# TensorE's program without loops, an earlier counter and another order of the last projection pass in a streaming encoder trunk

## The chip, the cores and the metric

The kernel runs on one core of a Trainium2 chip. Its engines are TensorE (PE; PEld is its weight load), VectorE (DVE), ScalarE (ACT), GpSimd (POOL) and SyncE (SP). The metric is the device time of one execution in microseconds (us); lower is better. TensorE's clock has two levels, 2.4 and 1.2 GHz; the profile gives the granted clock as a share of the higher one.

## What is computed

One layer of a streaming encoder for 640 tokens (512 of a prompt, 8 streams of 16), model width 2048, all in float32. Cut to what matters:

```python
xn = rms_norm(x, norm_mix_g)
glu, qkv, b_raw, a_raw, z, gates = split(xn @ w_in)
y_conv = silu(layer_norm(causal_dwconv(glu_a * sigmoid(glu_b)) + b)) @ conv_pw2
o, s_new = gated_delta_chunked(q, k, v, beta, g, s_prev, chunk)   # per 64 or 16 tokens
y_dn = (rms(o) * silu(z)) @ dn_w_o
x = x + (sigmoid(g0) * y_conv + sigmoid(g1) * y_dn) @ w_out       # the projection
xn = rms_norm(x, norm_ffn_g)
s = (xn @ w_q) . sub_keys; top 16 of 16 x 16 pairs, 8 heads       # the router
x = x + sum_k gelu(xn . u[idx_k]) * gate_k * v[idx_k]             # 16384 experts
y = rms_norm(x, norm_final_g)
```

## The kernel before, in words

Each engine has its own hand-written program; they meet only at semaphores, which count upwards. A float32 product is made of three passes of a rounded format: the operand's high part (`hi`, a copy by ScalarE) and low part (`lo`, the difference, by GpSimd or VectorE), multiplied high by high, high by low and low by high. So behind most matmuls stands a chain: a load by SyncE, `hi` on ScalarE, `lo` on GpSimd or VectorE, then TensorE.

The kernel goes through four stages.

1. **Input projections and convolutions** (from 59 us to about 690 us on TensorE): `pe.Fori(0, NC)`, L498, 8 iterations of five groups q, k, v, gate, glu, 480 matmuls of 320 columns each. `product` (L489) issues them. Then the gates' products go on as filler work.
2. **The gated delta rule**: `pe.Fori(0, PT)`, L694, 4 iterations. `delta` issues the small matmuls of one tile of 128 tokens, and `gates(n)` puts n filler matmuls between them. A last tile, for the streams, is written out behind the loop.
3. **Merge, projection, router.** `merge_half` (L1659, L1663) makes y_conv and y_dn, in a loop at L1670; VectorE's `merge` (L1929, L1931, L1935) combines them into the rows `mhi` and `mlo`, 16 rows in all, and raises `mg_out` (at L1931) and `m_lo` (at L1935). The projection goes over 8 column blocks of 256 (`oc`), two halves of the inner dimension (`kh`) and five token tiles (`t`): 7 blocks in the loop at L1692, in the order kh, high parts of all t, low parts of all t; the eighth block behind it (`for t`, L1730 and on) in the order t, kh. Its weight halves `whi[kh]`, `wlo[kh]` are one buffer each: half 0 is free again after `w_done`, half 1 after the block's last low part (`wo_mm`); ScalarE's `weight` (L1806) fills `whi` and raises `w_hi`, GpSimd (L2231) fills `wlo` and raises `w_lo`. VectorE's `add` (L1949) adds a bank to x and raises `wo_add`, which TensorE asks for before it writes that bank again. So that the first block passes, VectorE raises `wo_add` by five itself, at L1942, behind its last merge: TensorE's first projection matmul stands behind all of VectorE's merges. The router is the loop at L1786: `query` and `scores` (L1759, L1749).
4. **Experts** (from 2345 us). First one-hot products `group` with the first table's units between them (loops at L2476 and L2481), then 32 chunks in `phase`. A chunk has 8 units; TensorE's unit is 24 matmuls of 384 columns (L2467, L2472) and then 2 x 10 of the second table (L2498 in float32; L2506, L2507, L2508 in three passes), whose low weights VectorE makes (`low_v`, L2744). `phases` (L2347 and on) writes chunk 1 alone, 14 chunks in a loop of 7 iterations (L2352), chunks 16 and 17 alone, 12 chunks in a loop of 6 iterations (L2357), and the last three alone. All engines have the same shape of program. VectorE and GpSimd also gather and weight single expert rows in it (L2806, L2771), and SyncE and ScalarE load both tables.

In a loop the value that a wait asks for stands in a register. `wreg`, `Stage.count` and `wait_count` therefore wait and then also raise a counter of their own:

```python
def wait_count(eng, name, s, v):
    eng.wait_ge(s, v)
    eng.sem_inc(pace2[name], 1)
```

Of the kernel before, what the change touches and what calls it, by code (L numbers as in the profile page):

```python
# [19 lines left out]
TILES = T // P  # L20
PT = NP_TOK // P
# [3 lines left out]
NC = CONV // P  # L25
# [11 lines left out]
NOC = D // OCW  # L37
# [32 lines left out]
CHUNKS = NK // ET  # L70
# [4 lines left out]
NU = 2 * ET  # L75
# [6 lines left out]
GLN, GTILE = 8, 6  # L82
NGU = H + 2 * KD
RAWMOVE = 2 * len(KINDS) * NC + 2 * GLN + 2


def build(nc, x_prompt, x_sample, consts, params, conv_prefix, dconv_prefix, state_in, w_ba, w_first, w_units,
          keys, ffn_g, final_g, peer_u, peer_v, u_units, v_units,
          y_prompt, y_sample, conv_new_p, dconv_new_p, state_new_p, conv_new_s, dconv_new_s, state_new_s):
    with ExitStack() as ctx:  # L90
# [95 lines left out]
        def wreg(eng, name, s, v):  # L186

            eng.wait_ge(s, v)
            eng.sem_inc(pace[name], 1)
# [19 lines left out]
        NPROJ = 2 * len(KINDS) * NC  # L209
# [245 lines left out]
        def _(pe):  # L455
# [39 lines left out]

            pe.wait_ge(x_hi, 2 * TILES)
            pe.wait_ge(x_lo, 2 * TILES)
            with pe.Fori(0, NC) as c:  # L498
                for i, kd in enumerate(KINDS):
                    if kd == "q":  # L500
                        pe.wait_ge(glu_done, c + 1)
                    elif kd == "v":
                        pe.wait_ge(norm_root["k"], c + 1)
                    elif kd == "gate":
                        pe.wait_ge(evac["q"], c + 1)
                    elif kd == "glu":
                        pe.wait_ge(evac["k"], c + 1)
                    for kh in range(2):
                        n = 2 * i + kh
                        pe.wait_ge(lo_done, c * 10 + (n + 1))  # L510
                        for th in range(2):
                            m = product(ps[PSK[kd]], n, kh, th, 0, 24)
                        m.then_inc(unit_done, 1)
                pe.wait_ge(sq_done["q"], c + 1)
                pe.wait_ge(norm_root["q"], c + 1)
                sum_rows(ps[3], at(SQ, T)).then_inc(mm_sum["q"], 1)
                pe.wait_ge(sq_done["k"], c + 1)
                pe.wait_ge(evac["v"], c + 1)
                sum_rows(ps[2], at(SQ + T, T)).then_inc(mm_sum["k"], 1)
# [171 lines left out]

            pe.wait_ge(ln_root, 1)
            pe.wait_ge(ln_mean, 1)
            with pe.Fori(0, PT) as t:  # L694
                gates, done = gate_steps(t * GTILE + GLN, t * (2 * GTILE) + (NPROJ + 2 * GLN), RAWMOVE, lambda s, v: wreg(pe, "pe", s, v))
                delta(t, False, lambda s, v: wreg(pe, "pe", s, v), lambda per, k: t * per + k, gates)
                assert done[0] == PER * GTILE, done
            gates, done = gate_steps(GLN + PT * GTILE, NPROJ + 2 * (GLN + PT * GTILE), RAWMOVE, lambda s, v: pe.wait_ge(s, v))
            delta(PT, True, lambda s, v: pe.wait_ge(s, v), lambda per, k: count_s(per, k), gates)
# [732 lines left out]
        class Stage:  # L1432
# [14 lines left out]
            def count(self, eng, name, s, v):  # L1447

                eng.wait_ge(s, v)
                eng.sem_inc(self.pace[name], 1)  # L1450

            def block(self):
                return self.run.enter_context(nc.Block())
# [191 lines left out]
        def _(pe, st=st):  # L1645
# [21 lines left out]
            merge_half(1, 1, 1, 1)  # L1667
            merge_half(2, 0, 0, 0, c_lo)
            merge_half(3, 1, 1, 0)
            with pe.Fori(1, MN // 2) as i:  # L1670
                for r in range(2):
                    st.count(pe, "pe", mg_out, 2 * i + r - 1)
                    for j in range(2):
                        merge_half(i * 4 + (2 * r + j), 2 * i + r, r, j)

            def weights(kh):
                return tuple(w[:, kh, :].rearrange("p (k c) -> p k c", k=8) for w in (whi, wlo))
# [11 lines left out]
            pe.sem_inc(wo_mm, TILES)  # L1689
            pe.wait_ge(m_lo, 8)  # L1690
            pe.wait_ge(mg_out, MN - 1)
            with pe.Fori(0, NOC - 1) as oc:  # L1692
                for kh in range(2):
                    wh, wl = weights(kh)
                    st.count(pe, "pe", w_hi, 2 * oc + kh + 1)
# [31 lines left out]
                        m = pe.transpose(ps[TR_BANK[n]][:, k * P:(k + 1) * P], x1[:, t, kk * P:(kk + 1) * P], ident)  # L1727
                    m.then_inc(n_tr, 1)

            for t in range(TILES):  # L1730
                pe.wait_ge(wo_add, (NOC - 1) * TILES + t + 1)
                for kh in range(2):
                    wh, wl = weights(kh)
                    pe.wait_ge(w_hi, EN - 1 + kh)
                    high(t, kh, wh)
                    pe.wait_ge(w_lo, EN - 1 + kh)
                    m = low(t, kh, wl)
                m.then_inc(wo_mm, 1)
                if t >= 2:
                    transpose(t - 2)  # L1740
            transpose(3)
            pe.wait_ge(iota_st, 2)

# [39 lines left out]
            query_rows(0, TCOLS[1:], 0, KD, False)  # L1783
            query_rows(0, TCOLS[1:], 0, KD, True).then_inc(q_mm, 1)
            query(0, 1, True)
            with pe.Fori(1, QN // 2) as i:  # L1786
                for r in range(2):
                    query(i, r, False)
            scores(QN - 1, 1)
# [118 lines left out]
        def _(v, st=st):  # L1908
            v.memset(nsm[:, 0, :], 0.0).then_inc(eps_set, 1)
            v.memset(nsm[:, 1, :], EPS).then_inc(eps_set, 1)  # L1910

            def split_low(lo, src, hi, i, s_hi, s_lo):

# [25 lines left out]
            with v.Fori(1, MN // 2) as i:  # L1939
                for r in range(2):  # L1940
                    merge(i * 2 + r, r, i * 4 + (2 * r + 2))
            v.sem_inc(wo_add, TILES)  # L1942
            v.wait_ge(xr_ld, 32)

            def add(oc, t):
# [361 lines left out]
        def wait_count(eng, name, s, v):  # L2307

            eng.wait_ge(s, v)
            eng.sem_inc(pace2[name], 1)  # L2310

        xg_ld, x1g_ld, iota_ready = sem2("xg_ld"), sem2("x1g_ld"), sem2("iota_ready")
        pre_ld, g0_ld, g_mul = [sem2(f"pre_ld{i}") for i in range(PRE)], sem2("g0_ld"), sem2("g_mul")
# [22 lines left out]
        NQ = NGG * NBB  # L2336
# [97 lines left out]
        def _(pe):  # L2434
# [38 lines left out]
                if 3 in quarters:  # L2473
                    mmi.then_inc(unit_free, 1)

            with pe.Fori(0, NU // 4) as i:  # L2476
                for u in range(4):
                    for g in range(4):
                        group(i * 16 + (u * 4 + g), g % 2)
                        first_table(i * 4 + u, u % 2, i * 2 + u // 2, u // 2, (g,))  # L2480
            with pe.Fori(0, (NQ - 4 * NU) // 2) as i:  # L2481
                for r in range(2):
                    group(i * 2 + (4 * NU + r), r)

            def phase(c, par, ut, vt, has_u):
                for j in range(NU):
# [4 lines left out]
                    for q in range(2):  # L2491
# [15 lines left out]
                            pe.matmul(out, vh, a_l, start=False, stop=False)  # L2507
                            mmi = pe.matmul(out, vl, a_h, start=False, stop=e == SPLIT - 1)  # L2508
                        mmi.then_inc(v_mm, 1)
            phases(pe, phase)  # L2510

            pe.wait_ge(v_add, CHUNKS * KD + 4)
            for t in range(DT):
# [489 lines left out]
```

## Time and profile before

| | |
|---|---|
| time, median of 3 executions | 4795.71 us (4790.95 to 4795.77) |
| the profiled execution | 4787.57 us |
| its span, first to last instruction | 4786.0 us |
| TensorE busy | 4548.3 us (95%), 28205 matmuls |
| VectorE busy | 3410.1 us (71%) |
| ScalarE, GpSimd busy | 1317.9 us, 1323.9 us |
| mean granted TensorE clock | 0.977 |
| fetched for TensorE's program (queue q8) | 136 packets, 2.23 MB |

Matmuls are pipelined, so a row's duration (0.3 us) is longer than the step from one matmul to the next. Idle time in front of an instruction is written behind its row, with what ended it; "issue" stands for time in which the engine waited for nothing that the profile shows. An engine name with a q behind it (DVEq, PEldq) is that engine's sequencer: its branches, register work and semaphore increments, which are not counted as busy.

### The profile page before, as it was taken

The numbers are of one execution on the slowest core, as the hardware profiler recorded it, in microseconds if no ns is written. First come the engines' busy times: TensorE is split into PE (matmuls) and PEld (weight loads), VectorE is DVE, ScalarE is ACT, GpSimd is POOL, SyncE is SP. The second block draws the span as 40 slices with busy tenths as digits, with TensorE's granted clock in tenths as the row PEclk, the third lists the DMA queues.
The fourth block names the chain that finished last, engine by engine and source line by source line (L and its number), as shares of the span: only waits on it lengthen the run. The fifth ranks groups of instructions, "written<-read, shape, count | busy, mean of one in ns | idle before, by whom it ended". The sixth has DMA issues, their size and how long they took to land. (4 is left out here: it accounts for less than half of the span.)

```text
span 4786.0 us, 84564 instructions
## 1 busy us (share of the span) xinstructions
PE 4548.3 (95%) x28205; PEld 4355.8 (91%) x28205; DVE 3410.1 (71%) x4571; ACT 1317.9 (28%) x2054; POOL 1323.9 (28%) x936
## 2 busy tenths in 40 slices
PE   8999989999999999999679999999999999999995
PEld 8999989999998999999678998999999999999994
DVE  4889872334443331068887988898899999999998
ACT  4232323222221221132372222222222222222222
POOL 0111132211222333333002333333333333333332
PEclk8999999999999999999899999999999999999998
DMA  3222323221224433221268999999999999999998
GB/s 119 86 87 85 88 66 98 72 70 59 73 76 155 138 115 141 88 111 65 76 221 327 370 368 356 367 367 363 364 372 380 381 376 374 378 378 374 377 377 329
DMA packets 283660, 1085.18 MB, mean 227 GB/s; under 512 B 23696, under 2 KB 104464, under 8 KB 209936
## 3 DMA queue, kind: packets, MB, share of 16 engines
q0 software_dynamic: 74752, 538.99, 28.7%
q1 hardware_dynamic: 168336, 400.91, 25.2%
q10 hardware_dynamic: 40320, 142.10, 7.6%
q8 instruction: 136, 2.23, 0.2%
q14 instruction: 116, 0.95, 0.1%
HBM read 1017.03 MB, written 64.88 MB: 226 GB/s over the span
## 5 line engine op out<-in xcount | busy, mean ns | idle before, releaser
L489 PE MATMUL ps<-xhi,hi 128*128 128x320 f32 x2560 | 773.8, 316 | 31.0 <-POOL lo L1391 15.7
L489 PE MATMUL ps<-xlo,hi 128*128 128x320 f32 x2560 | 761.8, 311 | 0.0
L2506 PE MATMUL ps<-ahi,vhi 128*128 128x384 f32 x1536 | 667.4, 434 | 45.7 <-DVE workr L2744 45.7
L2467 PE MATMUL ps<-xhi,whi 128*128 128x384 f32 x2048 | 691.9, 338 | 9.3 <-issue 9.3
L2467 PE MATMUL ps<-xlo,whi 128*128 128x384 f32 x2048 | 688.3, 336 | 0.0
L2580 ACT ACTIVATE whi<-work 128x1024 fp32r<-128x1024 f32 x240 | 254.6, 1061 | 1519.5 <-PE ps L2472 1429.0
L2806 DVE CUSTOM_DVE_ANT_0 work<-work,keep 128x2048 f32<-128x2048 f32 x256 | 585.2, 2286 | 33.1 <-DMA work<-in_peer_u,cur_u 21.8
L2771 DVE SCALAR_TENSOR_TENSOR keep<-work,act_w,keep 128x2048 f32<-128x2048 f32 x256 | 600.7, 2346 | 4.5 <-DMA work<-in_peer_v,cur_v 3.0
L2870 POOL DMA_INDIRECT work<-in_peer_v,cur_v x256 | 369.7, 1444 | 757.6 <-DVE keep L2771 729.5
L2507 PE MATMUL ps<-alo,vhi 128*128 128x384 f32 x1536 | 521.1, 339 | 0.0
L2508 PE MATMUL ps<-ahi,workr 128*128 128x384 f32 x1536 | 520.9, 339 | 0.0
L489 PEld LDWEIGHTS ps<-xhi,hi 128*128 128x128 f32 x2560 | 485.2, 190 | 36.2 <-POOL lo L1391 16.2
L489 PEld LDWEIGHTS ps<-xlo,hi 128*128 128x128 f32 x2560 | 485.3, 190 | 2.9 <-issue 2.9
L2870 POOL DMA_INDIRECT work<-in_peer_u,cur_u x256 | 248.0, 969 | 721.8 <-DVE hid L2806 696.2
L489 PE MATMUL ps<-xhi,lo 128*128 128x320 f32 x2560 | 441.9, 313 | 0.0
L2724 DVE TENSOR_TENSOR wlo<-work,whi 128x1024 fp32r<-128x1024 f32 x240 | 293.8, 1224 | 172.4 <-ACT whi L2580 156.0
L1391 POOL TENSOR_TENSOR lo<-keep,hi 128x1024 fp32r<-128x1024 f32 x80 | 211.1, 2639 | 695.9 <-ACT hi L720 685.5
L2506 PEld LDWEIGHTS ps<-ahi,vhi 128*128 128x128 f32 x1536 | 291.9, 190 | 122.1 <-issue 57.3
L2498 PE MATMUL ps<-aT,work 128*128 128x384 f32 x992 | 402.4, 488 | 0.2 <-issue 0.2
L2472 PE MATMUL ps<-xhi,wlo 128*128 128x384 f32 x2048 | 398.7, 335 | 0.0
L2467 PEld LDWEIGHTS ps<-xhi,whi 128*128 128x128 f32 x2048 | 386.0, 188 | 10.1 <-issue 10.1
L489 PEld LDWEIGHTS ps<-xhi,lo 128*128 128x128 f32 x2560 | 391.6, 189 | 1.0 <-issue 1.0
(336 smaller groups left out, 8188.9 us busy)
## 6 DMA issues: line engine op xcount, KB each, us to landing
work<-in_v_units ACTq DMA_DIRECT2D x256, 512.0 KB, 8.2
work<-in_u_units SPq DMA_DIRECT2D x240, 512.0 KB, 8.2
keep<-in_w_first SPq DMA_DIRECT2D x160, 512.0 KB, 3.6
keep<-in_w_units SPq DMA_DIRECT2D x32, 1024.0 KB, 4.9
gates_dram<-work SPq DMA_DIRECT2D x8, 3072.0 KB, 11.8
gbuf<-gates_dram SPq DMA_DIRECT2D x31, 768.0 KB, 10.2
arena<-in_w_units SPq DMA_DIRECT2D x32, 512.0 KB, 4.1
gates_T<-keep SPq DMA_DIRECT2D x32, 320.0 KB, 2.2
```

The costliest lines, as they stand in the source:

```text
L489: m = pe.matmul(out[:, o:o + HT], w[:, k, :], x[:, 8 * kh + k, c], start=kh == 0 and i == 0, stop=kh == 1 and i == 23)
L2467: pe.matmul(out, h3[:, k, :], (xlo if m % 2 else xhi)[:, 8 * half + k, :], start=half == 0 and m == 0, stop=False)
L2472: mmi = pe.matmul(out, l3[:, k, :], xhi[:, 8 * half + k, :], start=False, stop=half == 1 and k == 7)
L2498: pe.matmul(out, w4[:, q, e, :], (a0 if is_first(c) else aT[1 - par])[:, e, :], start=e == 0, stop=False)
L2506: pe.matmul(out, vh, a_h, start=False, stop=False)
L2507: pe.matmul(out, vh, a_l, start=False, stop=False)
L2508: mmi = pe.matmul(out, vl, a_h, start=False, stop=e == SPLIT - 1)
L2580: act.activation(whi[:, r, :], uraw[r], ACT.Copy).then_inc(hi_done, 1)
L2724: v.tensor_tensor(wlo[:, r, :], uraw[r], whi[:, r, :].bitcast(F32), ALU.subtract).then_inc(lo_done, 1)
L2771: v.scalar_tensor_tensor(x1g[:, t, :], row, act_w2[:, j:j + 1], x1g[:, t, :], ALU.mult, ALU.add).then_inc(v_used, 1)
L2806: v.tensor_tensor_reduce(out=row, in0=row, in1=xg[:, ut, :], scale=1.0, scalar=0.0, op0=ALU.mult, op1=ALU.add, accum_out=hid[:, j:j + 1]). ...
L2870: pool.indirect_dma_start(out=dst, out_offset=None, in_=table, in_offset=bass.IndirectOffsetOnAxis(ap=cur, axis=0)).then_inc(ld, 16)
```

## The change

Two edits. In the first, all nine loops of TensorE's program are written out by Python's `range`; the other engines keep theirs. The waits' values are then plain numbers, and for these `Stage.count` and `wait_count` no longer raise the pace counter. In the experts' stage TensorE no longer uses `phases`. In the second, VectorE raises `wo_add` by five at the head of its program for stage 3 and not behind its merges, and the projection's last block takes tiles 0 and 1 together: both with half 0 of the weights, then both with half 1.

```diff
-            with pe.Fori(0, NC) as c:
+            for c in range(0, NC):
...
-            with pe.Fori(0, PT) as t:
-                gates, done = gate_steps(t * GTILE + GLN, t * (2 * GTILE) + (NPROJ + 2 * GLN), RAWMOVE, lambda s, v: wreg(pe, "pe", s, v))
-                delta(t, False, lambda s, v: wreg(pe, "pe", s, v), lambda per, k: t * per + k, gates)
+            for t in range(0, PT):
+                gates, done = gate_steps(t * GTILE + GLN, t * (2 * GTILE) + (NPROJ + 2 * GLN), RAWMOVE, lambda s, v: pe.wait_ge(s, v))
+                delta(t, False, lambda s, v: pe.wait_ge(s, v), lambda per, k: t * per + k, gates)
...
                 eng.wait_ge(s, v)
-                eng.sem_inc(self.pace[name], 1)
+                if type(v) is not int:
+                    eng.sem_inc(self.pace[name], 1)
...
-            with pe.Fori(1, MN // 2) as i:
+            for i in range(1, MN // 2):
...
-            with pe.Fori(0, NOC - 1) as oc:
+            for oc in range(0, NOC - 1):
...
-            for t in range(TILES):
-                pe.wait_ge(wo_add, (NOC - 1) * TILES + t + 1)
-                for kh in range(2):
-                    wh, wl = weights(kh)
-                    pe.wait_ge(w_hi, EN - 1 + kh)
-                    high(t, kh, wh)
-                    pe.wait_ge(w_lo, EN - 1 + kh)
-                    m = low(t, kh, wl)
-                m.then_inc(wo_mm, 1)
-                if t >= 2:
-                    transpose(t - 2)
+            def last_half(t, kh):
+
+                wh, wl = weights(kh)
+                pe.wait_ge(w_hi, EN - 1 + kh)
+                if kh == 0:
+                    pe.wait_ge(wo_add, (NOC - 1) * TILES + t + 1)
+                high(t, kh, wh)
+                pe.wait_ge(w_lo, EN - 1 + kh)
+                m = low(t, kh, wl)
+                if kh:
+                    m.then_inc(wo_mm, 1)
+
+            last_half(0, 0)
+            last_half(1, 0)
+            last_half(0, 1)
+            last_half(1, 1)
+            for t in range(2, TILES):
+                last_half(t, 0)
+                last_half(t, 1)
+                transpose(t - 2)
...
-            with pe.Fori(1, QN // 2) as i:
+            for i in range(1, QN // 2):
...
             v.memset(nsm[:, 1, :], EPS).then_inc(eps_set, 1)
+            v.sem_inc(wo_add, TILES)
...
-            v.sem_inc(wo_add, TILES)
             v.wait_ge(xr_ld, 32)
...
-            with pe.Fori(0, NU // 4) as i:
+            for i in range(0, NU // 4):
...
-            with pe.Fori(0, (NQ - 4 * NU) // 2) as i:
+            for i in range(0, (NQ - 4 * NU) // 2):
...
-            phases(pe, phase)
+            for c in range(1, CHUNKS + 1):
+                phase(c, c % 2, None, None, c < CHUNKS)
```

## Rows read from the trace of the kernel before

**Rows 1.** The page: busy time of the engines over the span
```profile
...
PE 4548.3 (95%) x28205; PEld 4355.8 (91%) x28205; DVE 3410.1 (71%) x4571; ACT 1317.9 (28%) x2054; POOL 1323.9 (28%) x936
```

**Rows 2.** What TensorE (PE) waited for: engine, line, releaser, us in total, times, longest
```profile
...
PE ps L2506 <- DVE workr L2744: 45.7, 15, 12.6
...
PE ps L2467 <- issue: 9.3, 3, 4.2
PE ps L1682 <- DVEq L1942: 8.1, 1, 8.1
...
PE ps L489 <- issue: 5.8, 3, 2.2
...
PE ps L1749 <- issue: 1.3, 6, 0.2
```

**Rows 3.** Loop-end branches of TensorE's sequencer, of three loops: duration ns min/median/max
```profile
...
L694 PEldq COMPARE_BRANCH  x4: 83/3616/4065, 942.0 to 1367.4; - x4
...
L2352 PEldq COMPARE_BRANCH  x7: 76/208/7036, 2723.5 to 3578.8; - x7
...
L2357 PEldq COMPARE_BRANCH  x6: 76/208/223, 3854.3 to 4543.3; - x6
```

**Rows 4.** Stretches of the experts' stage: us; busy us of five engines; clock; DMA share
```profile
...
2865.10:3009.90 144.80, 139.88 (x738) 130.44 (x737) 126.52 (x128) 36.08 (x65) 47.61 (x40) 0.99 0.95 359
3292.40:3436.10 143.70, 139.45 (x737) 130.71 (x736) 126.94 (x128) 35.95 (x65) 50.51 (x40) 0.99 0.96 365
3578.80:3716.60 137.80, 137.80 (x738) 129.35 (x737) 126.77 (x128) 36.11 (x65) 50.22 (x40) 1.00 0.98 378
```

**Rows 5.** DMA queue of TensorE's instructions: whole span, then 3578.8 to 3854.3 us
```profile
...
q8 instruction: 136, 2.23, 0.2%
...
q8 instruction: 13, 0.21, 0.3%
```

**Rows 6.** TensorE's timeline: start, us, instruction, idle before it and releaser
```profile
...
1087.86 0.38 PE L489 MATMUL ps<-xhi,hi 128*128 128x320 f32 x1 [2.22 <-issue]
...
1809.17 0.55 PE L1682 MATMUL ps<-d_whi,d_mhi 128*128 128x256 f32 x1 [8.06 <-DVEq L1942]
...
2019.48 1.22 PE L1686 MATMUL ps<-d_wlo,d_mhi 128*128 128x256 f32 x8 [2.20 <-POOL d_wlo L2231]
...
2876.98 0.41 PE L2506 MATMUL ps<-ahi,vhi 128*128 128x384 f32 x1 [3.57 <-DVE workr L2744]
...
3299.98 0.41 PE L2467 MATMUL ps<-xhi,whi 128*128 128x384 f32 x1 [4.25 <-issue]
...
3442.67 0.41 PE L2467 MATMUL ps<-xhi,whi 128*128 128x384 f32 x1 [3.09 <-issue]
```

**Rows 7.** Timelines of ACT, DVE and POOL around the projection's first and last pass
```profile
...
1799.19 1.92 ACT L1806 ACTIVATE d_whi<-keep 128x2048 fp32r<-128x2048 f32 x1 [6.75 <-DMA keep<-in_w_units]
...
1802.97 3.82 DVE L1931 TENSOR_TENSOR arena<-arena 128x640 f32<-128x640 f32 x1
...
1808.86 1.91 ACT L1806 ACTIVATE d_whi<-keep 128x2048 fp32r<-128x2048 f32 x1 [1.22 <-DVE d_mlo L1935]
...
1811.12 4.59 POOL L2231 TENSOR_TENSOR d_wlo<-keep,d_whi 128x2048 fp32r<-128x2048 f32 x1 [5.02 <-ACT d_whi L1806]
...
2014.88 4.56 POOL L2231 TENSOR_TENSOR d_wlo<-keep,d_whi 128x2048 fp32r<-128x2048 f32 x1 [9.80 <-ACT d_whi L1806]
```

**Rows 8.** Two stretches behind TensorE's longest wait, columns as in Rows 4
```profile
...
1809.00:1812.50 3.50, 3.33 (x15) 3.36 (x16) 0.00 (x0) 1.77 (x1) 1.38 (x1) 0.50 1.02 433
1812.50:1815.00 2.50, 2.50 (x22) 2.50 (x22) 0.00 (x0) 0.00 (x0) 2.50 (x1) 0.99 1.01 419
```

**Rows 9.** VectorE's timeline at three loop starts of the experts' stage
```profile
...
2873.36 0.17 DVE L2760 TENSOR_TENSOR act_w<-act_w,sel 128x8 f32<-128x8 f32 x1 [3.45 <-issue]
...
3302.47 1.02 DVE L2744 TENSOR_TENSOR workr<-work,vhi 128x384 fp32r<-128x384 f32 x2
...
3445.44 1.02 DVE L2744 TENSOR_TENSOR workr<-work,vhi 128x384 fp32r<-128x384 f32 x2
```

More of the change, by code:

```diff
@@ L2309, in wait_count @@
             eng.wait_ge(s, v)
-            eng.sem_inc(pace2[name], 1)
+            if type(v) is not int:
+                eng.sem_inc(pace2[name], 1)
         xg_ld, x1g_ld, iota_ready = sem2("xg_ld"), sem2("x1g_ld"), sem2("iota_ready")
```

## The prediction

> **What bounds the kernel now.** I read the page first: TensorE is busy 4548.3 of 4786.0 us, the next engine 3410 [rows 1]. So only two things shorten the kernel: time in which TensorE stands still, and time in which it runs at the lower clock. The next view is the list of what TensorE waited for [rows 2]. The reader is to see that few of its entries have to do with loops: 9.3 us in three pieces and 5.8 us in three pieces under "issue", which is the sequencer itself; 1.3 us in six pieces under "issue" in the router; and 8.1 us at L1682, whose releaser is VectorE's sequencer at L1942, the increment that the change moves. The largest entry, 45.7 us for VectorE's low weights at L2744, is work and not program.
>
> The third view is the loop-end branch [rows 3]. TensorE's program has nine loops and 47 taken branches. A normal one takes 208 ns, while matmuls already handed over go on running, and no idle time stands behind it: in the last loop of the experts' stage all five are 208 to 223 ns, and its stretches are 137.8 us. Only six branches are long. Three are the three taken ones of the delta rule's loop (median 3.6 us, longest 4.1), three are in the first experts' loop (up to 7.0 us). They are the six "issue" pieces above.
>
> The fourth view is what straight code costs, and the trace holds that comparison already. Chunks 16 and 17 and their neighbours are written out: from 3578.8 to 3854.3 us 13 packets of TensorE's instructions were fetched [rows 5], and TensorE was busy 137.80 of 137.80 us in the stretch shown [rows 4]; the looped stretches behind it, without a fetch for TensorE, take 137.8 too. Straight and looped code run alike apart from the six branches.
>
> **The change part by part.**
>
> *Loops of the delta rule.* It removes three long branches: 5.8 us of idle time [rows 2], 2.22 of it in front of the matmul at 1087.86 [rows 6]. Behind that one the clock fell to the lower level for 3.4 us. What such a fall costs: at clock 0.50 TensorE started 15 matmuls in 3.5 us, at 0.99 then 22 in 2.5 us [rows 8], so 3.4 us at half rate lose about 1.5 to 1.7 us. Together 7.3 us. The work behind the branch is filler gate products whose weights are ready, and the small matmuls that need VectorE come 38 matmuls (5.6 us) later, so I take nothing off; the bounds are 4 and 7.5.
>
> *Loops of the experts' stage.* Three branches with 9.3 us of idle time go. But here something is late next. VectorE's program keeps its loop, and at its loop start it too stands under "issue" for 3.1 to 3.7 us before L2760 [rows 9], in every iteration. Where TensorE's branch was short, that alone made TensorE wait: 3.57 us in front of 2876.98 for L2744 [rows 6], and that iteration took 144.8 us, longer than the 143.7 with a 7 us branch in it [rows 4]. So I work out when the low weights would be asked for. A unit is 137.8 / 16 = 8.61 us, and 26 of its 46 matmul records come before the first low weights: 4.9 us. At 3299.98 TensorE had been free since 3295.73; it would ask at 3300.6. The first of VectorE's two pieces at 3302.47 ends at 3303.0, and TensorE starts 0.3 us later: a wait of 2.7 instead of 4.25 us, gain 1.5. At 3442.67 in the same way: free at 3439.6, asks at 3444.5, gets them at 3446.3, a wait of 1.8 instead of 3.09, gain 1.2. The third (free at 2727.0, weights at 2732.5) gains 0.8. The clock falls after either wait. Sum 3.5 us; the bounds are 0 and 9.3 plus two clock falls, 12.5.
>
> A rule of the Trainium skill can be held against these rows. Runtime: NRT & Kernel Launch, section Instruction fetch mechanics, says that a taken branch whose target lies outside a window of two blocks of 256 instructions forces a fetch before execution goes on, and names this as a reason to unroll. Four of TensorE's loops have bodies longer than that, with 21 taken branches; at the 2.5 us that the six cost on average the rule would give 53 us. The rows show 15 us, from six branches only, so the sum goes by the rows.
>
> *The other seven loops, the register waits and the pace counters.* A wait on a register is three steps of TensorE's sequencer and a constant one at most one, but the sequencer is ahead of the matmuls everywhere except where it waits for data. The cover is TensorE's queue of matmuls already issued. What remains is the router's 1.3 us in six pieces [rows 2]; I take 0.6, between 0 and 1.3. In the one-hot loops before the experts VectorE works without a break, so nothing is gained there.
>
> *The counter raised early.* At 1801.1 the merge's last matmul has been issued and the first weights are there (ScalarE's copy from 1799.19 takes 1.92 us, [rows 7]). TensorE then idles 8.06 us until VectorE's increment [rows 6]. What is late next? Tiles 0 to 3 need nothing more, 64 matmuls at 0.12 us are 7.7 us, until 1809. Tile 4 writes a bank that VectorE's last merge reads; its sum at 1802.97 ends at 1806.8. The low weights of half 0 were begun by GpSimd at once and take 4.6 us. Half 1 is asked for at 1801.2 + 14.4 = 1815.6 and is copied by 1810.8, its low part at 1825.2 and ready at 1815.7 [rows 7]. Nothing is late, so 8.0 us go, and with them the 3.5 us at clock 0.50 behind the idle time [rows 8], another 1.5. Sum 9.5 us; the bounds are 6 and 9.5. VectorE's increment at the head of its program is one sequencer step ahead of its first subtraction, under 0.1 us.
>
> *The last pass.* TensorE asked for half 1's low weights after two thirds of tile 0 and idled 2.20 us until 2019.48 [rows 6]; GpSimd made them from 2014.88 in 4.56 us [rows 7], and could not begin before half 1 was free, so they are due at 2019.4 after the new order too. The new order puts 24 matmuls (2.9 us) of tile 1 ahead, which moves the request from 2017.1 to 2020.0, 0.6 us behind the weights. Idle time 2.3 and one clock fall 1.5: 3.8 us. Against it, tile 0 is finished 0.5 us later than now, but its norm has until tile 2 is done. From tile 1 on everything is earlier by the full amount, the wait for the last tile's norm and transposes moves with it. The bounds are 1 and 4.
>
> Sum: 7.3 + 3.5 + 0.6 + 9.5 + 3.8 = 24.7 us. The profiled execution took 4787.57 us, which gives 4762.9. The median of the three timed runs stands 8.1 us above it; taken off the median, the sum gives 4771.0, and that is my number.
>
> **The rivals.**
>
> *Slower: every further packet of instructions costs TensorE.* 136 packets are fetched now. In the straight stretch there were 13 packets to about 2950 records of weight loads and matmuls; 56410 records make some 250, so about 110 more, half of them where the DMA engines are busy 0.95 to 0.98 of the time [rows 4]. 0.3% of 16 engines over 275.5 us is 1.0 us for each packet [rows 5]. If each delayed TensorE by that, 110 us would be lost against 24.7 gained: 4881. It decides from 0.22 us a packet on. Against it: 13 packets in that same full stretch cost nothing. For it only that packets and data share the engines. Chance 0.05.
>
> The same page of the Trainium skill calls crossing a block mostly hidden; by that, and by the trace, this rival is weak.
>
> *The removed waits come back.* In the experts' stage VectorE's own loop start takes all of the gain, the delta rule's chain takes 2 us, and the projection's first pass finds its weights late. Gain 8 to 16 us, 4780 to 4788. For it: in such loops VectorE is nearly always close behind. Chance 0.22.
>
> *No difference.* The early part's gain is lost where loads and gathers set the pace, at 2510 to 3160 us, with DMA shares to 0.98. Then only what lies behind remains, some 3 us: 4793. Against it: the loads there are issued when buffers come free, and so move with the engines. Chance 0.05.
>
> *More.* VectorE's loop start also shortens once TensorE no longer fetches beside it; then both clock falls and 9.3 us go: a gain of 34, and up to 10 more from its 45.7 us: 4752 to 4762. Chance 0.08.
>
> **How the numbers follow.** The forecast case (gain 17 to 32, 4764 to 4779) has 0.60. This kernel's measurement can tell about 0.2%, 9.6 us, from no change. Faster by more than that are the forecast, the case of more, and three quarters of the case in which waits come back: 0.84. The same: the rest of that and the case of no difference, 0.11. Slower 0.05. The range takes in more and the returning waits, and 3 us for the spread of medians: 4752 to 4789.
>
> **What would show it.** In the new profile: no "issue" entries at L489 and L2467; no L1942 entry, TensorE's first L1682 matmul within 1 us of the merge's end; no wait for POOL L2231 at the last pass; a clock that stays up at these places; new or longer waits at L2506 for VectorE's L2744 where the three branches were; stretches of 137.8 us in the second half as now; some 240 packets for TensorE, about 3.9 MB. It would be wrong if idle time under "issue" appeared in straight code, if the stretches from 3.6 ms on were longer than 137.8 us, or if the merge and projection waited on weights.

## The result, and the profile after

The changed kernel takes 4738.33 us (median of three runs, 4717.75 to 4740.88) against 4795.71 us: a ratio of 0.9871, with a 95% interval of 0.9828 to 0.9914. That is 57 us less. I had forecast 4771, in a range of 4752 to 4789: the direction was right, and the gain was more than twice what I had summed, below the range. A second measurement of the same kernel gave 4730.66 us and 0.9891 [0.9857, 0.9926].

The first view is the page of the kernel after, parts 1 and 3 (queue, kind, packets, MB, share).

```profile
...
PE 4534.7 (96%) x28205; PEld 4346.2 (92%) x28205; DVE 3411.9 (72%) x4571; ACT 1317.7 (28%) x2054; POOL 1282.6 (27%) x936
...
q8 instruction: 223, 3.65, 0.3%
q14 instruction: 104, 0.85, 0.0%
```

TensorE's instructions take 223 packets where they took 136 [rows 5]. Queue 14, which fetches for the other engines, has 104 packets and had 116. So what the other engines fetch became less too, though no loop of theirs was touched: the pace edit takes increments out of their programs as well. That second number was the one to look at.

The second view is what TensorE waited for after the change (line, releaser, us in total, times, longest).

```profile
PE ps L2517 <- DVE workr L2756: 31.7, 12, 12.0
...
PE ps L489 <- POOL lo L1391: 5.5, 1, 5.5
```

The entries under "issue" at L489, L2467 and L1749 and the one for VectorE's increment are gone [rows 2]; a single entry under "issue" is left, 0.9 us in the one-hot products. The experts' low weights make 31.7 us where they made 45.7 [rows 2], although I expected more waits there. And the wait at L489 for a low product of GpSimd is 5.5 us in one piece; before it was 15.7 us in two, the longer one 10.2. I had not looked at that entry.

The third view is the experts' stage of the kernel after in two stretches of the same 738 matmuls (us; busy us of the five engines; clock; DMA share; GB/s).

```profile
2841.10:2978.90 137.80, 137.80 (x738) 129.31 (x737) 127.40 (x131) 36.09 (x64) 47.56 (x40) 1.00 0.97 378
3259.40:3397.20 137.80, 137.80 (x738) 129.31 (x737) 126.99 (x129) 36.11 (x65) 49.02 (x40) 1.00 0.98 377
```

Before, two such stretches of the first half took 144.8 and 143.7 us [rows 4]. These two take what only the second half took; experts 1, a stage of the table below, still has some waits for VectorE's low weights, 2.1 us in this profile and 9.6 in a second one.

The fourth view is TensorE's timeline of the kernel after, where the projection begins.

```profile
1780.50 0.36 PE L1683 MATMUL ps<-d_whi,d_mhi 128*128 128x256 f32 x1 [0.64 <-ACT d_whi L1816]
```

0.64 us of idle time stands where 8.06 us stood [rows 6]. At the last pass no wait is left.

Where the time went is read best by stage. Every kernel here issues the same 28205 matmuls, so a stage can be cut at the same matmul, by its number in order, in each trace. The table gives the length of each stage in the profiled executions. "conv" is the end of the first stage, behind its loop; "experts 1" runs from 2529.6 to 3564.7 us of the kernel before, so it holds nearly all of the first experts' loop; "router" holds the query products ahead of it.

```
us                before  after  after_again   e1      e2      e3      e4      e5      e7      e10
first loop         630.2  628.9    631.4     628.0   632.6   630.2   632.1   629.1   631.9   628.4
conv                82.5   68.1     81.1      82.5    82.5    82.5    82.3    68.1    68.0    69.1
delta rule         812.3  806.7    803.7     805.1   815.3   812.3   812.2   806.6   806.5   814.9
merge              247.2  247.3    247.2     247.3   247.3   247.1   247.1   247.3   247.3   247.2
projection         306.9  296.4    296.4     307.0   307.1   299.6   303.3   296.5   307.1   306.9
router             265.9  260.7    260.7     264.9   263.1   266.0   266.0   260.7   260.7   265.6
one-hot            184.5  182.7    183.2     185.8   184.5   184.5   184.4   183.2   182.9   184.3
experts 1         1035.1 1004.6   1015.3    1020.2  1022.9  1039.7  1037.0  1037.5  1008.0  1034.1
experts 2          973.5  975.0    978.8     973.5   999.5   973.5   976.3   973.9   980.5   992.3
end                212.4  210.5    212.0     212.9   213.4   211.6   213.9   211.3   211.0   218.1
```

Of the 69.8 us between the two profiled executions, experts 1 gives 30.5, conv 14.4, the projection 10.5, the delta rule 5.6, the router 5.2. The profiled execution of the kernel after was the fastest of its three.

### The profile page after: what moved, and what is told of

It reads as the page before. It is cut to its first block and busy times, and to the rows that moved or that the text cites. A ratio compares the mean times of both kernels' runs of the same rounds, so it can differ in the third digit from the quotient of the medians.

```text
span 4716.1 us, 80323 instructions
## 1 busy us (share of the span) xinstructions
PE 4534.7 (96%) x28205; PEld 4346.2 (92%) x28205; DVE 3411.9 (72%) x4571; ACT 1317.7 (28%) x2054; POOL 1282.6 (27%) x936
## 5 line engine op out<-in xcount | busy, mean ns | idle before, releaser
L489 PE MATMUL ps<-xhi,hi 128*128 128x320 f32 x2560 | 771.2, 315 | 14.5 <-DVE arena L1196 8.9
L489 PE MATMUL ps<-xlo,hi 128*128 128x320 f32 x2560 | 759.2, 310 | 0.0
L2517 PE MATMUL ps<-ahi,vhi 128*128 128x384 f32 x1536 | 667.6, 435 | 31.7 <-DVE workr L2756 31.7
L2882 POOL DMA_INDIRECT work<-in_peer_v,cur_v x256 | 358.5, 1401 | 763.3 <-DVE keep L2783 720.4
L489 PEld LDWEIGHTS ps<-xhi,hi 128*128 128x128 f32 x2560 | 483.2, 189 | 18.8 <-DVE arena L1196 10.1
L489 PEld LDWEIGHTS ps<-xlo,hi 128*128 128x128 f32 x2560 | 483.2, 189 | 2.9 <-issue 2.9
L489 PE MATMUL ps<-xhi,lo 128*128 128x320 f32 x2560 | 440.0, 311 | 0.0
L489 PEld LDWEIGHTS ps<-xhi,lo 128*128 128x128 f32 x2560 | 389.4, 188 | 1.0 <-issue 1.0
L1391 POOL TENSOR_TENSOR lo<-keep,hi 128x1024 fp32r<-128x1024 f32 x80 | 198.7, 2484 | 688.1 <-ACT hi L720 677.8
L2478 PEld LDWEIGHTS ps<-xlo,whi 128*128 128x128 f32 x2048 | 384.6, 188 | 0.0
```

The source lines that it names most:

```text
L489: m = pe.matmul(out[:, o:o + HT], w[:, k, :], x[:, 8 * kh + k, c], start=kh == 0 and i == 0, stop=kh == 1 and i == 23)
L2478: pe.matmul(out, h3[:, k, :], (xlo if m % 2 else xhi)[:, 8 * half + k, :], start=half == 0 and m == 0, stop=False)
L2517: pe.matmul(out, vh, a_h, start=False, stop=False)
L2882: pool.indirect_dma_start(out=dst, out_offset=None, in_=table, in_offset=bass.IndirectOffsetOnAxis(ap=cur, axis=0)).then_inc(ld, 16)
```

## The experiments

Each median stands beside the runs of the kernel before on the same chip. On the first chip, e1 to e4, those have the median 4788.8 us; on the second, the kernel after once more and e5 to e7, 4789.95; on the third, e8 to e11, 4792.64. Apart from the kernel after, each version has one profile only, and the stages swing from profile to profile: the two of the kernel after differ by 10.7 us in experts 1 and by 13 us in conv.

**e1: the loops alone.** All nine loops written out, everything else as before.

```diff
-            with pe.Fori(0, PT) as t:
+            for t in range(0, PT):
...
-            phases(pe, phase)
+            for c in range(1, CHUNKS + 1):
+                phase(c, c % 2, None, None, c < CHUNKS)
```

> Only TensorE's nine loops written out; every engine keeps its pace counters, so the programs of VectorE, ScalarE and GpSimd are those of before, word for word. Theory 1 (VectorE's program sits differently against its fetch blocks because 116 semaphore steps fell out of its straight code ahead of the experts' first loop; TensorE's loops alone give what the prediction worked out): VectorE still stands under 'issue' for 3 to 3.7 us before L2760 at each of the seven iterations, TensorE waits 1.5 to 3.6 us for L2744 there, and the gain is 8 to 15 us. Theory 2 (TensorE's loops are the cause of all of it, because its block fetches beside VectorE's made VectorE late): VectorE's 'issue' entries before L2760 are gone and the gain is 30 us or more, most of it between the experts' start and chunk 15.

Measured: 4775.39 us, 0.9976 [0.9962, 0.9990]. The delta rule and the experts gain, but TensorE's straight program alone is a fifth to a quarter of the change. VectorE's stall at its loop start stays. The view is what VectorE waited for from 2583 to 4600 us, in this kernel:

```profile
...
DVE act_w L2761 <- issue: 19.6, 6, 3.6
```

and in the kernel before:

```profile
...
DVE act_w L2760 <- issue: 19.8, 6, 3.7
```

This is what the prediction took as given: six starts of VectorE's loop, 3.3 us each.

**e2: the pace counter alone.** No increment where the number waited for is plain; TensorE's loops stay.

```diff
-                eng.sem_inc(self.pace[name], 1)
+                if type(v) is not int:
+                    eng.sem_inc(self.pace[name], 1)
```

> Only the edit that a wait on a plain number no longer raises the pace counter, in the programs of all engines; TensorE keeps its loops, the projection is as before. Theory 1 (VectorE's shorter straight code): VectorE's 'issue' entries before L2760 (19.8 us in 6 pieces before) vanish or fall to below 5 us, TensorE's waits for L2744 in the experts' stage fall by 15 to 20 us, TensorE's own long branches may change too, since its straight code gets shorter as well, and the gain is 15 to 35 us. Theory 2 (TensorE's loops): no change within 0.2%, all these entries stay.

Measured: 4792.53 us, 1.0010 [0.9994, 1.0026]. No difference in the time, but the profile is not the same at all. VectorE's entry at L2762 is gone and experts 1 is 12 us shorter; experts 2 is 26 us longer (its profiled execution, 4805.0 us, was the slowest of its twelve). The views are what TensorE waited for from 2583 to 4640 us, and its branch at the end of the second experts' loop (ns, min/median/max).

```profile
...
PE ps L2469 <- issue: 15.7, 5, 3.4
...
PE ps L2500 <- issue: 2.7, 3, 1.5
```

```profile
...
L2359 PEldq COMPARE_BRANCH  x6: 76/6098/6391, 3845.0 to 4559.9; - x6
```

In the kernel before, that branch is never over 223 ns [rows 3]. The first loop's branch, up to 7.0 us there, has 208 ns at most here. The bodies of the loops are as long as before (1664 records of TensorE between two branches), and what the edit changed is how much code stands ahead of them. So it does two things at once: it shortens the programs, and it moves every loop against the 16 KB packets in which TensorE's program is fetched. And experts 1 still has 13.3 us of waits for VectorE's low weights, without a long branch of TensorE or the stop at L2762: its two longest, 5.5 and 4.7 us, each stand behind a wait of ScalarE for a load, of 15.6 and 14.9 us.

**e3: the counter raised early, alone.**

```diff
+            v.sem_inc(wo_add, TILES)
...
-            v.sem_inc(wo_add, TILES)
```

> Only the projection's counter raised at the head of VectorE's program. Both theories: TensorE's 8.06 us of idle time in front of the first L1682 matmul fall below 1 us and the half clock behind them goes, 9 to 9.5 us in the profile; the rest of the profile stays as before, VectorE's program having one step moved and none less. If the gain is above 15 us, the increment's place changed something else.

Measured: 4787.53 us, 1.0005 [0.9991, 1.0019]. The wait goes as forecast; what TensorE waited for from 1700 to 2030 us:

```profile
...
PE ps L1686 <- POOL d_wlo L2231: 2.2, 1, 2.2
PE ps L1682 <- ACT d_whi L1806: 0.4, 1, 0.4
```

The projection is 7.3 us shorter in the profile, experts 1 is 4.6 us longer, with six long branches of TensorE (18.1 us) where the kernel before has three (9.3 us). TensorE's program in this kernel is that of the kernel before, word for word: so the number of long branches is not set by its code alone. Of the 7.3 us nothing can be told in the time.

**e4: the last pass in its new order, alone.** The edit is the function `last_half` of the change.

> Only the last pass of the projection in the new order. The wait of 2.20 us for GpSimd's L2231 goes with the half clock behind it, 3.8 us; a gain of 0 to 4 us, hardly to be told from no change. If the norm's chain behind it held TensorE back, the waits at L1727 and L1759 (8.6 us before) would grow by as much.

Measured: 4791.07 us, 1.0002 [0.9986, 1.0017]. The wait for L2231 is gone, the projection is 3.6 us shorter, and again experts 1 is 1.9 us longer with six long branches (18.4 us). Alone, e2, e3 and e4 are each worth nothing that can be measured.

**The kernel after, once more.**

> The changed kernel itself, once more, beside the others on one chip. If the 57 us hold, the ratio is 0.985 to 0.989; if its first three executions were lucky, above 0.990. All theories expect the profile as before it: no 'issue' entry of TensorE in the experts' stage, none of VectorE before its act_w2 product, no GpSimd low product above 4 us behind the first loop.

Measured: 4730.66 us, 0.9891 [0.9857, 0.9926]; its six runs lie from 4721.34 to 4766.13. The profiled one took 4746.54, with conv at 81.1 us instead of 68.1. So the 14 us of conv are not a part of the change that every execution shows.

**e5: the kernel after, with VectorE's program moved back.** The edit puts 116 increments that nobody waits for into VectorE's program behind the projection: as many as the pace edit took out of it ahead of the experts' first loop. TensorE's program is that of the kernel after.

```diff
+            for _ in range(116):
+                v.sem_inc(st.pace["dve"], 1)
```

> The changed kernel with 116 empty semaphore steps in VectorE's program, in a place where VectorE stands idle for 15 us (ahead of the projection's first add), so that everything behind them sits against the fetch blocks as in the kernel before. Theory 1 (position against the fetch blocks): VectorE's 'issue' entries of 3 to 3.7 us at the experts' first loop are back, TensorE waits for L2756 there, and the experts' stage is 10 to 20 us longer than in the changed kernel. Theory 2 (VectorE was late because TensorE's loops were there): no such entries, time as the changed kernel's.

Measured: 4754.89 us, 0.9928 [0.9900, 0.9955], 24 us above the kernel after on the same chip. The two intervals overlap, but each ratio lies outside the other's interval. What VectorE waited for from 2583 to 4600 us, and TensorE over the same stretch:

```profile
...
DVE act_w L2774 <- issue: 18.6, 6, 3.6
```

```profile
...
PE ps L2519 <- DVE workr L2758: 21.4, 11, 6.1
```

The stall is back, six times and 3.1 us each, and behind it TensorE waits 21.4 us for the low weights, where the kernel after waits 1.8 us in that stretch. In its second profile, the kernel after waits 11.6 us there. Experts 1 is 1037.5 us, within 3 us of the kernel before (1035.1), although TensorE has no branch at all, and 22 to 33 us longer than in the kernel after. So the stop at L2774 comes and goes with the length of the code ahead of VectorE's loop. But not all of the stage's loss is its doing: three of TensorE's waits, 12.3 of the 21.4 us, stand behind waits of ScalarE for a load (13.2 to 16.3 us), as three do in the second profile of the kernel after. Such late loads come in profiles with and without the stops, and no run was made to test them. e1, with TensorE's straight program and the same six stops but no such load in the loop, has 1020.2 us in experts 1, against 1004.6 to 1008.0 in the kernel after, e7 and e8: 12 to 16 us is my estimate of what the stops cost in that stage.

The kernel after is not free of stops at that place either. Its own view from 2583 to 4600 us still has, at the first operation behind the loop's start:

```profile
...
DVE wlo L2736 <- issue: 10.2, 6, 2.1
```

VectorE's sequencer stands twice at the loop's start in the kernel before: 5.3 to 7.3 us right behind the branch (4.7 where the loop ends and the branch is not taken), and 3.8 to 4.5 us a little later. The first is in every kernel here in which VectorE has that loop, 5.2 to 5.9 us in the kernel after, and most of it lies under work already handed over; the second is the one that went.

**e6: the kernel before, with VectorE's program moved on** by 140 such increments, so that its loop lies elsewhere while TensorE's program stays. 140 more is 256 away from 116 less, which the expectation takes for the same position.

> The kernel before with 140 empty semaphore steps at the same place of VectorE's program: 140 more or 116 less is the same position against blocks of 256 instructions. Theory 1: VectorE's 'issue' entries before L2760 vanish; TensorE keeps its own long branches, so that the stage gains 5 to 15 us. Theory 2: the entries stay, no change within 0.1%.

Measured: 4784.13 us, 0.9993 [0.9971, 1.0015]. From 2583 to 4600 us VectorE's entry at the loop start is gone and TensorE's is there:

```profile
...
PE ps L2469 <- issue: 11.9, 4, 3.1
PE ps L2508 <- DVE workr L2746: 3.3, 2, 2.8
```

VectorE's entry at the first stop, L2726, is 10.9 us in six, much as in the kernel after. The wait for the low weights shrinks to 3.3 us, and TensorE's own branches take 11.9, four long ones now. Experts 1 is 1026.2 us, 8.9 less than before, and the time shows no difference. With e1 this says that either stall alone holds the stage up; both have to go.

**e7: loops and pace counter together,** the projection as before.

> TensorE's loops written out and the pace counters left out for plain numbers, the projection as before. Theory 1 (the two parts work only together: each one alone leaves the other engine's loop stall, and the 15.9 us GpSimd product goes only when both change TensorE's step): gain 40 to 48 us, the 15.9 us product gone. Theory 2 (the parts add up): the sum of the two runs alone, 12 us for the loops and -4 for the counters, so 5 to 12 us, the 15.9 us product still there.

Measured: 4748.09 us, 0.9922 [0.9896, 0.9947]. e1 gave 0.24% and e2 nothing; together they give 0.78%. So with TensorE's loops written out, the pace edit is worth 0.54%, some 26 us, and the intervals of e1 and e7 do not overlap. In the profiles that is 14.5 us in conv, 12.2 in experts 1 and 4.2 in the router, less 7.0 in experts 2. The router gains 5.2 us here, against 1.0 in e1 and 2.8 in e2. The kernel after adds the projection's edits to e7 and is 17 us faster on the same chip, with intervals that overlap; by stage they are worth 10.7 us.

**e8: the experts' loops of the other engines written out as well.**

```diff
-            with eng.Fori(0, HALF // 2 - 1) as i:
...
+            for c in range(1, CHUNKS + 1):
+                phase(c, c % 2, int(c > HALF), None if c == 1 else int(c > HALF + 1), c < CHUNKS)
```

> The changed kernel with the 32 chunks of the experts' stage written out in the programs of all five engines, so that no engine has a loop end there. Theory 1 (what is lost in that stage are loop ends, of TensorE and of VectorE alike, and straight code costs nothing): VectorE's last 'issue' entries there (10 to 12 us in 6 to 7 pieces) vanish, the stage from the first chunk to chunk 15 falls by 5 to 15 us and its scatter with it; ratio to the kernel before 0.985 to 0.988. Rival (fetching straight code for five engines beside 0.98 of DMA load delays one of them): new 'issue' entries in the second half, where 12 chunks now take 137.8 us a pair, and a longer time than the changed kernel's.

Measured: 4719.37 us, 0.9856 [0.9835, 0.9876]; five runs from 4716.76 to 4729.01. From 2583 to 4600 us TensorE waits for nothing, and VectorE has one entry, without "issue":

```profile
...
DVE wlo L2726 <- ACT whi L2582: 158.2, 203, 2.4
```

Now the stage depends on no loop's position: both of VectorE's stops are gone, and experts 1 is 1005.7 us. It has the lowest median of all versions, but e9 and e11 can't be told from it, and against the kernel after the medians from two chips differ by 11 us and the intervals overlap.

**e9, e10, e11: GpSimd let in.** The 10.2 us wait at L489 that the kernel before has and the kernel after hasn't comes from one low product of GpSimd. GpSimd's timeline of the kernel before, and VectorE's beside it:

```profile
...
684.52 15.91 POOL L1391 TENSOR_TENSOR lo<-keep,hi 128x1024 fp32r<-128x1024 f32 x1 [8.15 <-ACT hi L720]
...
679.32 18.91 DVE L1218 SCALAR_TENSOR_TENSOR arena<-arena,par 128x880 f32<-128x880 f32 x18
698.26 2.71 DVE L1228 TENSOR_TENSOR keep<-arena 128x512 f32<-128x512 f32 x1
```

The same product in the kernel after, and VectorE's row there:

```profile
...
681.99 2.56 POOL L1391 TENSOR_TENSOR lo<-keep,hi 128x1024 fp32r<-128x1024 f32 x1 [6.92 <-ACT hi L720]
...
676.97 23.29 DVE L1218 SCALAR_TENSOR_TENSOR arena<-arena,par 128x880 f32<-128x880 f32 x16
```

15.91 us against 2.56 for the same instruction. In the kernel before it ends only when VectorE's row of 18 operations of 1.05 us has run out at 698.26; in the kernel after three products fall inside a row of 16, of which three take 3.3 us and the others 1.1. The edit gives VectorE one wait in the middle of the row for the product that GpSimd is about to make; e9 is the kernel after with it, e10 the kernel before, e11 is e8 with it.

```diff
+                    if not more and j == 18:
+                        v.wait_ge(lo_done, NPROJ + 5)
```

> The changed kernel with one wait more in VectorE's program: in the last convolution iteration, ahead of tap 18, it waits until GpSimd's fifth low product of that stretch is done, so that the two engines don't start at once. Theory 1 (the 15.9 us product is GpSimd shut out by VectorE's unbroken row of two-input operations, and whether that happens is settled within 0.1 us at the start, differently from execution to execution of the changed kernel): no product above 4 us in any profile, the slow executions (4745 to 4766) disappear from the timed ones, median 0.1 to 0.2% under the changed kernel's. Rival (the long product is something of GpSimd's own): it still shows in some profile, median the same.

> The same wait in the kernel before, where six profiles of six with its loops or its counters showed the 15.9 us product. Theory 1: the product takes 2.4 to 3.3 us, TensorE's wait of 10.2 us for L1391 and the half clock behind it go, gain 12 to 15 us (ratio 0.997). Rival: product and time as before.

> Both on top of the changed kernel: the experts' stage straight for all engines, and VectorE's one wait. If both theories hold, the effects add up: 10 to 25 us under the changed kernel, ratio to the kernel before 0.983 to 0.987. If either fails, the one that holds alone shows here.

Measured: e9 4722.96 us, 0.9857 [0.9837, 0.9877]; e10 4787.97 us, 0.9991 [0.9979, 1.0004]; e11 4724.02 us, 0.9861 [0.9838, 0.9884]. GpSimd's and VectorE's timelines of e10:

```profile
...
682.44 2.66 POOL L1393 TENSOR_TENSOR lo<-keep,hi 128x1024 fp32r<-128x1024 f32 x1 [7.88 <-ACT hi L720]
...
685.13 18.01 DVE L1220 SCALAR_TENSOR_TENSOR arena<-arena,par 128x880 f32<-128x880 f32 x13 [2.31 <-POOL lo L1393]
```

VectorE gives up 2.31 us, the product takes 2.66, and conv falls from 82.5 to 69.1 us: the cause of the long product and what it costs in its stage are shown. Yet e10's time hardly moves. In its profile, taken of the slowest of its twelve runs, experts 2 is 18.8 us longer. What TensorE waited for from 2583 to 4600 us in e10:

```profile
...
PE ps L2508 <- DVE workr L2746: 18.3, 5, 7.3
PE ps L2469 <- issue: 15.5, 5, 4.0
```

The five long branches lie in experts 1, which is no longer than before. Experts 2 has no long branch, but 14.2 us in two waits for VectorE, near 3.60 and 3.81 ms, and ahead of each ScalarE waits 17.0 and 17.5 us for a load; why those loads are late no run tells.

On the kernel after, conv is near 69 us in e9 and e11 alike, and all nine of their runs lie between 4718.38 and 4727.15, where the kernel after spread from 4717.75 to 4766.13, on other chips. That the wait is what narrowed the spread is not shown: e8 without it lies as close (4716.76 to 4729.01). And e11 is no faster than e8, so the two effects did not add up as expected.

## Why the prediction was wrong, by its own steps

*Loops of the delta rule:* right. 7.3 us forecast, and the stage is 7.2 us shorter in e1. In the kernel after it is 5.6 us shorter in the profile where conv is short, with a new wait of 1.2 us for VectorE at its start, and 8.6 in the profile where conv is long.

*The counter raised early:* 9.5 forecast, 7.3 in e3. The first wait behind it is 0.4 us for ScalarE's weights, and 0.64 in the kernel after, as described; the term was 2 us too large. *The last pass:* 3.8 forecast, 3.6 in e4. Together 10.5 us against 13.3.

*The other seven loops, register waits and pace counters:* 0.6 us forecast, with 1.3 as the bound, and 5.2 us in the router alone. My cover, that TensorE's sequencer is ahead of its matmuls, did not hold there. The six pieces under "issue" (1.3 us) go in e1; the longest wait of the router, at L2449, goes from 30.6 to 28.2 us in e2; the rest is 0.3 us of another wait and some 1.2 us in which TensorE is busy.

*Loops of the experts' stage, and the pace counters:* these are the steps that failed. I wrote that VectorE's loop keeps its "issue" of 3.1 to 3.7 us "in every iteration" (2.9 to 3.7 in the six starts) and so takes most of the gain, and got 3.5 us, at most 12.5. Measured were 30.5 us in experts 1 (19.8 in the second profile of the same kernel). For the loops alone the time agrees: e1 is exactly that case, with VectorE's six stalls, and my terms for it (7.3, 3.5 and 0.6) make 11.4 us, or 0.24%, which is what its runs gave. That it agrees so closely is luck, as the interval spans 5 to 18 us and the profiled execution, among its fastest, shows 14.9 us in experts 1 where I had 3.5. What I missed is in the other edit. I priced the pace counter as steps of TensorE's sequencer that nothing waits for, within the 0.6 us above; e7 against e1 puts it at some 26 us. It also takes 116 increments out of VectorE's straight code ahead of the loop, and that moved the loop to where one of the two stops at its start is gone: the 19.8 us at L2760 fell to none, e5 put 116 back and 18.6 us with them, and e6 made them vanish in the kernel before by moving its loop on. The six profiles with the longer code all have the six stops, and the six with the loop elsewhere have none. Of the 30.5 us in experts 1, e1 has 14.9 by TensorE's loops alone; the rest is about what I put the stops at, 12 to 16 us.

*The rule of the Trainium skill.* It forecast 53 us for TensorE's long loops. (By the records between two branches five loops are longer than 512, not four, the fifth being the one at L2476 with 788, so my count should have been 22 branches and 55 us.) The runs show far fewer long branches. The delta rule's loop, 2250 records, has a long one each time in all six kernels that keep it; the experts' loops, 1664 records, have some; loops of up to 991 records have none. In the first experts' loop there are three in the kernel before (9.3 us), six in e3 and e4 (18.1 and 18.4 us), four in e6 and five in e10, and in e3, e6 and e10 TensorE's program is that of the kernel before, word for word. In e2, where it is shorter, the first experts' loop has none and the second has five of five. So the position of the code seems to say which loop can have them, and something else how many; what that is, or whether it changes from one execution to the next, no run tells. By the Trainium skill, Runtime: NRT & Kernel Launch, section Instruction fetch mechanics, such a stall is what a taken branch out of the window of two blocks costs, and it is one reason to unroll; what a long branch costs is as these rows show, but how often it is long does not follow the rule. I was right to go by the rows for the sum of TensorE, and wrong not to ask what sets them: the same question would have led to VectorE's loop.

*What no step held:* GpSimd's product in conv; the stage is about 13 us shorter when it is short. In the profiles it was long in seven (before, e1 to e4, e6, the kernel after once more) and short in four (the kernel after, e5, e7, e8); with the wait added it was never long in three.

*The rivals.* Slower by packets fell: 87 more packets, some 240 to 250 in all forecast and 223 found, and TensorE busy without a gap in the two stretches shown, at DMA shares of 0.97 and 0.98. The removed waits come back: not in the kernel after; e1, the loops alone, has a gain of the size that this rival forecast. No difference: fell, as the experts' stage kept its gain. "More" was the nearest in time, at 4752 to 4762, and had the right sign and place. Its reason, that VectorE's loop start shortens once TensorE no longer fetches beside it, is refuted by e1: TensorE straight, VectorE's stall 19.6 us.

*Open.* What decides whether GpSimd's product gets in: in all seven long cases it starts 55.3 to 55.6 us behind the loop's end, in all four short ones 54.1 to 54.3, but why the kernels with the old loops are always late by that 1.2 us no run tells. The start alone does not settle it either: in e9 to e11 it is as late as in the long cases, and the product is short. And e3's and e4's gains in the projection, 7.3 and 3.6 us in the profile, are missing from their times; the longer experts 1 of their profiles takes back 4.6 and 1.9 of them. Nor does any run tell why loads come late in some profiles of the experts' stage, up to 17.5 us of waiting for ScalarE.

## What to carry to other kernels

An edit that removes instructions from an engine's straight code moves every loop behind it, and with it a stop of 3 to 7 us at the loop's start can come or go; so look in the profile of each engine for "issue" in front of the first instruction of a loop body, and compare the packets of all instruction queues. Where such a stall stands on the critical path, write out that loop on every engine on that path: TensorE alone gained 0.24% here, and 0.78% once the pace edit had also removed VectorE's stall (and, in the profile, the long product in conv). Judge parts together as well as one by one, since three edits that were each worth nothing made up most of the gain of the whole.

## What the hardware showed that I had not expected

A GpSimd operation of 2.5 us took 15.9 us beside a row of VectorE operations with two inputs in SBUF: in seven of eleven profiles it did not slip in between two of them, stayed out for 13.7 us, 13 operations, and ended 2.2 us after the row. Other products of the same kind get in behind one operation, beside the same row. Where it does get in, it is the VectorE operation that waits. The Trainium skill, SBUF — State Buffer, section SBUF: two separate sides, says that the two engines share ports under an exclusive lock that is held for a whole instruction. The trace agrees that one engine is shut out completely, but the loser lost not one instruction's time but thirteen. One wait in VectorE's row, 2.3 to 2.4 us, cured it in all three kernels.

Straight code cost TensorE no idle time that can be seen: from 2583 to 4600 us of the kernel after 86 packets of 16 KB were fetched for it, with the DMA engines busy 97 and 98% of the time in the stretches shown, and it waited 1.8 us in all, each time for VectorE.
